# Half of the weight products of a two-layer encoder turned over: activations stationary, 512 weight columns streaming

## The reference: what is computed

```
for i in range(2):
    h = rmsnorm(x, norm_mix_g[i])
    x = x + (even_mixer(h, ...) if i == 0 else diff_attention(h, ...))
    x = x + square(relu(rmsnorm(x, norm_ffn_g[i]) @ w_ff1[i])) @ w_ff2[i]    # 2048 -> 8192 -> 2048
return rmsnorm(x, norm_final_g)
```

## Time and profile before

| what | us |
|---|---|
| median of 3 runs (2211.26 to 2212.45) | 2212.16 |
| the profiled execution's own time | 2212.59 |
| its span in the trace | 2210.8 |
| busy: PE (matmul) / DVE / ACT / POOL | 2182.3 / 1525.7 / 1034.5 / 29.8 |

### The profile page before, as it was taken

One profiled execution on the slowest core, in us unless ns is written; L12 is line 12 of the kernel. 1 busy time (PEld: TensorE's weight loads), 2 busy tenths in 40 slices (PEclk: granted clock), 3 DMA queues, 4 the chain that ended last, 5 costly groups with the idle time before them and its releaser, 6 DMA issues.

```text
span 2210.8 us, 36913 instructions
## 1 busy us (share of the span) xinstructions
PE 2182.3 (99%) x12668; PEld 1909.4 (86%) x12668; DVE 1525.7 (69%) x2296; ACT 1034.5 (47%) x1466; POOL 29.8 (1%) x33
## 2 busy tenths in 40 slices
PE   6999999999999999999999999999999999999998
PEld 5888888888888888888888888888888888888887
DVE  7777767765665675677777777777656656756764
ACT  4444445543443453455545455555434434534553
POOL 3000000000000000000000000000000000000000
PEclk9999999999999999999999999999999999999999
DMA  8444445555555555555544444555555555555552
GB/s 287 171 162 163 170 168 207 197 191 188 190 190 190 189 186 190 182 187 191 185 172 172 163 164 167 173 189 190 190 190 181 192 187 182 189 190 189 190 190 95
DMA packets 64455, 405.65 MB, mean 183 GB/s; under 512 B 6631, under 2 KB 15847, under 8 KB 16396
## 3 DMA queue, kind: packets, MB, share of 16 engines
q1 hardware_dynamic: 61182, 401.06, 50.8%
q10 hardware_dynamic: 2846, 2.82, 0.4%
q0 software_dynamic: 368, 0.99, 0.1%
HBM read 402.70 MB, written 2.14 MB: 183 GB/s over the span
## 4 chain that ended last, share of the span: by engine, by line
issue 78%; PE 20%; DVE 1%; DMA 0%; ACT 0%; POOL 0%; POOLq 0%; SPq 0%; DVEq 0%; ACTq 0%
PE acc L973 12%; PE acc L976 6%; PE ps_scores L1015 0%; DMA x<-xT_dram 0%; PE ps_o L1015 0%; PE ps_aux L1083 0%; PE ps_attn_t L1047 0%; DVE gx L614 0%; ACT gx L341 0%; DVE w_lo L553 0%; PE ps_scores L1070 0%; POOL rstd_col L287 0%; PE ps_v L1036 0%; ACT w_hi L315 0%; POOL bias L212 0%
## 5 line engine op out<-in xcount | busy, mean ns | idle before, releaser
L553 DVE TENSOR_TENSOR w_lo<-raw,w_hi 128x1024 fp32r<-128x1024 f32 x752 | 917.9, 1225 | 321.5 <-ACT w_hi L315 306.9
L973 PE MATMUL acc<-gx,w_hi 128*128 128x512 f32 x3440 | 1088.9, 398 | 10.3 <-DVE gx L614 9.7
L315 ACT ACTIVATE w_hi<-raw 128x1024 fp32r<-128x1024 f32 x752 | 795.7, 1058 | 617.5 <-PE acc L976 613.9
L973 PE MATMUL acc<-mid,w_hi 128*128 128x512 f32 x2544 | 800.1, 396 | 0.3 <-DVE mid L911 0.3
L976 PEld LDWEIGHTS acc<-gx,w_lo 128*128 128x128 f32 x3440 | 648.2, 188 | 153.0
L976 PE MATMUL acc<-gx,w_lo 128*128 128x256 f32 x3440 | 678.1, 279 | 0.0
L976 PEld LDWEIGHTS acc<-mid,w_lo 128*128 128x128 f32 x2544 | 477.9, 188 | 112.9
L973 PEld LDWEIGHTS acc<-gx,w_hi 128*128 128x128 f32 x3440 | 526.4, 189 | 14.3 <-DVE gx L614 8.9
L976 PE MATMUL acc<-mid,w_lo 128*128 128x256 f32 x2544 | 499.8, 278 | 0.0
L973 PEld LDWEIGHTS acc<-mid,w_hi 128*128 128x128 f32 x2544 | 387.6, 189 | 0.8 <-DVE mid L911 0.7
L322 ACT ACTIVATE copied<-acc 128x256 f32<-128x256 f32 x215 | 81.8, 380 | 353.6 <-PE acc L976 349.3
(11 more groups left out here) (123 smaller groups left out, 538.3 us busy)
## 6 DMA issues: line engine op xcount, KB each, us to landing
raw<-weights_dram SPq DMA_DIRECT2D x375, 1024.0 KB, 4.8
x<-xT_dram SPq DMA_DIRECT2D x4, 512.0 KB, 9.2
bias<-bias_line SPq DMA_DIRECT2D x2, 1024.0 KB, 7.2
bias<-bias_line ACTq DMA_DIRECT2D x2, 1024.0 KB, 10.8
out_dram<-bias SPq DMA_DIRECT2D x3, 384.0 KB, 2.9
raw<-weights_dram SPq DMA_DIRECT2D x2, 512.0 KB, 6.2
bias<-bias_line SPq DMA_DIRECT2D x2, 512.0 KB, 6.9
pos_dft<-position_dft_dram POOLq DMA_DIRECT2D x1, 512.0 KB, 8.2
```

Source lines behind the costliest of these rows:

```text
L315: act.activation(w_hi[:, n % RING, :], raw[:, u % RAW_SLOTS, part * HALF:(part + 1) * HALF], ACT.Copy).then_inc(hi_ready, 1)
L553: dve.tensor_tensor(w_lo[:, n % RING, :], raw[:, u % RAW_SLOTS, part * HALF:(part + 1) * HALF], w_hi[:, n % RING, :].bitcast(F32), ALU.sub ...
L973: pe.matmul(acc_of(u)[:], w_hi[:, n % RING, cols], operand[:, kt, :], start=kt == 0, stop=False)
```

## The change

188 of the 376 units are done the other way round: the values of both attentions, both output projections and the down half of both feed-forwards. Such a unit is a quarter of a group of 512 output columns (4 k-tiles x 512 columns, again 1 MB). The activations are stationary, 128 tokens at a time, and the weights stream, 512 columns; each of two banks receives 128 tokens by 512 features:

```
+            def wide_half(n, part, q, operand, banks, o=0, free=(), between=(), done=None, order=range(KT)):
+
+                pe.wait_ge(lo_ready, n + 1 - N0 + 2 * o)
+                for t in range(QT):
...
+                    for i in range(2):
+                        at = 4 * q + 2 * part + i
+                        tile, cols = order[at], slice(i * WIDE, (i + 1) * WIDE)
+                        hi, lo = (operand[:, tile, a * SEQ + t * P:a * SEQ + (t + 1) * P] for a in range(2))
+                        pe.matmul(banks[t], hi, w_hi[:, n % RING, cols], start=at == 0, stop=False)
+                        pe.matmul(banks[t], hi, w_lo[:, n % RING, cols], start=False, stop=False)
+                        ins = pe.matmul(banks[t], lo, w_hi[:, n % RING, cols], start=False, stop=at == KT - 1)
```

The residual x is token-major, `x[P, QT, D]`. A group of 512 columns is added to it from two banks by two DVE instructions, and its squares are summed along the row by ACT. For the three inner norms PE turns the group, and ACT and DVE write gx from the turned tiles:

```
-                    dve.tensor_tensor(x[:, t, :], x[:, t, :], acc_of(u)[:, 0:SEQ], ALU.add).then_inc(acc_half, 1)
-                    dve.wait_ge(acc_half, r + 1 + r_o)
-                    dve.tensor_tensor(x[:, t, :], x[:, t, :], acc_of(u)[:, SEQ:], ALU.add).then_inc(acc_free, 1)
+                        dve.tensor_tensor(x[:, t, columns(g)], x[:, t, columns(g)], banks[g][t], ALU.add
+                                          ).then_inc(x_done, 1)
...
+                act.activation(squares_out, x[:, t, columns(g)], ACT.Square, accum_out=token_parts[:, t, g:g + 1]
...
+            def turn_group(n, group, g):
+                    for j in range(WIDE // P):
+                        cols = slice((WIDE // P * g + j) * P, (WIDE // P * g + j + 1) * P)
+                        for t in range(QT):
+                            ins = pe.transpose(turned_tile(j)[:, t * P:(t + 1) * P], x[:, t, cols], ident[:])
```

The opening is another product: the values of heads 0 to 3, k-tile by k-tile, so that each step needs one tile of x and one 128x512 piece of the weights. Twelve matmuls on ones stand ahead of it. The token-major x is loaded after units 4 and 5, and its squares stand on ACT between the splits of unit 5:

```
+            for c, (lo, hi) in enumerate(CHUNKS):
+                sp.dma_start(raw_open[:, lo:hi, :], opening[:, lo:hi, :]).then_inc(open_landed[c], 16)
+                if c > 1:
+                    sp.dma_start(x_first[:, lo:hi, :], x_fm[:, lo:hi, :]).then_inc(x_landed[c], 16)
+            load(4)
+            load(5)
+            for t in range(QT):
+                sp.dma_start(x[:, t, :], x_tok[:, t, :]).then_inc(tokens_landed[t], 16)
...
+            split_hi(8)
+            split_hi(9)
+            first_squares(0)
+            split_hi(10)
+            first_squares(1)
+            split_hi(11)
...
+            for _ in range(WARM):
+                pe.matmul(ps_aux[:, 0:P], ones[:], ones[:], start=True, stop=True)
+            for kt in range(KT):
+                pe.wait_ge(gx_ready, kt + 1)
+                pe.wait_ge(open_lo, kt + 1)
+                for t in range(QT):
...
+                    pe.matmul(v_banks[0][t], hi, w, start=kt == 0, stop=False)
+                    pe.matmul(v_banks[0][t], hi, w_rest, start=False, stop=False)
+                    ins = pe.matmul(v_banks[0][t], lo, w, start=False, stop=kt == KT - 1)
```

More of the change, by code:

```diff
@@ new lines, in wide_stage @@
+            def wide_stage(u0, g0, n, last=()):
+                for g in range(COL_GROUPS):
+                    for q in range(4):
+                        u = u0 + 4 * g + q
+                        if g == 0:
+                            quarter(u, **last[q])
+                        elif q == 0 and n is not None:
+                            quarter(u, first=[squares(n, g0 + g - 1, g - 1)], second=[turned_hi(n, g - 1)])
+                        else:
+                            quarter(u)
@@ L499, in _, with group @@
-            feed_forward(act, 0, U_FF0, hidden, output, last_output(N_MIX1))
-            unit(U_QKV1)
-            unit(U_QKV1 + 1)
-            def squares(h, oh=0):
-                def step():
-                    act.wait_ge(o_ready, A_HEADS + h + 1 + oh)
-                    act.wait_ge(osq_done, QT * (h + oh))
+                narrow(u, w, o, ow, second=[hi_hidden])
+            def group(u, G, g, m, w, o=0, oG=0, om=0):
+                for q in range(4):
+                    quarter(u + q, o)
@@ new lines, in _ @@
+            end = C_HEADS - 1
+            wide_stage(U_OUT1, G_OUT1, N_FFN1,
+                       (dict(first=[exps(1, A_HEADS + 2 * end + 1, HEADS - 1)]), dict(first=[copy_attn(HEADS - 1)]),
+                        dict(before=[o_squares(end)], first=[hi_att1(end)]), none))
+            norm_end(N_FFN1, G_OUT1 + COL_GROUPS - 1)
+            feed_forward(act, 1, hidden, group)
+            for g in range(COL_GROUPS):
+                for q in range(4):
+                    u = UNITS - KT + 4 * g + q
+                    quarter(u, first=[squares(N_FINAL, G_LAST + g - 1, g - 1)] if g and q == 0 else [], split=u + 2 < UNITS)
@@ L628, in clear_sum, with narrow @@
-            def clear_sum(m=None):
-                if m is not None:
-                    dve.wait_ge(mid_ready, m)
-                dve.memset(sum_sq[:], 0.0).then_inc(sum_steps, 1)
-            def unit(u, evac, o=0, before=(), first=(), then=(), second=(), split=True):
+            def narrow(u, w, evac, o=0, before=(), first=(), second=()):
+                for step in before:
+                    step()
+                split_lo(2 * u + 4, o)
+                for step in first:
+                    step()
+                evac()
+                split_lo(2 * u + 5, o)
+                for step in second:
+                    step()
@@ L635, in unit, with quarter @@
+            def quarter(u, o=0, before=(), first=(), second=(), split=True):
                 for step in before:
@@ new lines, in quarter @@
+            def quarter(u, q, operand, banks, done, o=0, free=(), tiles=None, middle=(), late=(), after=(),
+                        order=range(KT)):
+                for part in range(2):
+                    if tiles is not None:
+                        ready, count = tiles
+                        pe.wait_ge(ready, count + 4 * q + 2 * part + 2)
+                    wide_half(2 * u + part, part, q, operand, banks, o, free if part == q == 0 else (),
+                              late if part else (), done if part == 1 and q == 3 else None, order)
+                    for step in after if part else middle:
+                        step()
```

1518 lines of the change are left out of this document (782 added, 736 removed).

## The result

| what | before | after |
|---|---|---|
| median of 4 runs each, us | 2212.01 (2211.26 to 2212.45) | 2180.60 (2180.37 to 2180.83) |
| ratio, 95% interval | | 0.9858 [0.9841, 0.9875] |
| span of the profiled execution | 2210.8 | 2178.6 |

The changed kernel is 31.4 us faster, 1.4%.

A forecast was written before the change was run, and what follows sets the result against it. PE's matmul stream, with an opening ahead and a tail behind, was taken as the bound. 2212.6 + 3.9 - 12.8 + 2.6 + 2.0 - 2.3 = 2206.0 us, forecast 2206, range 2184 to 2216.

The forecast's parts named there:

- wide products: 188 of 376 units made wide: 24 matmuls of 512 columns at an assumed 0.2331 us each, +3.9 us.
- opening and its waits: Start of the kernel: opening ends at 31 us, then three waits; 11.9 us lost against 24.7, so -12.8.
- small matmuls: On PE: 96 transposes added, 56 turn_v transposes and 16 sum-of-squares matmuls gone, +2.6 us.
- new waits: PE waits on lo_attn in 11 heads, 1 us, and at U_QKV1, 1 us: +2.0 us.
- the end: Last matmul's start to end of span: 10.2 us against 12.5, so -2.3.
- Rival (a): Wide products: a cost per matmul, 512 columns take 0.2290, dropping 1504 matmuls gains 14.5 us, giving 2187.6; chance 0.2.
- the sixteen-row: Row of sixteen 256-column matmuls in succession, 0.119 us each; used for the wide products' lower price, cited for (a).
- (b): Wide products: the 512-column stream from the ring costs 0.236 us, +13.1 us, giving 2219; chance 0.1.
- (c): Opening: clock stays at 1.2 GHz throughout, it ends near 49 us and gains nothing, giving 2219; chance 0.08.
- (d): Wide products: (a)'s mechanism at a quarter of its size, 512 columns take 0.2314 us, giving 2198; chance 0.05.
- The one at U_QKV1: PE waits for the second residual addition before U_QKV1 may start, 1 us.
- The 0.1 in eleven heads: lo_attn, now behind the second split, is 0.1 us late in 11 heads, 1 us in all.

The follow-up runs named there:

- experiment 2: Kernel before, with all eight 512-column w_hi products of a half unit, then its eight 256-column w_lo products, instead of two and two: 2218.04 us (1.0025).
- Experiments 4 and 5: Kernel before, each k-tile pair on mid as three 512-column products, weights streaming (first) or activations streaming (second): 2191.85 and 2191.68 us (both 0.9908).
- Experiment 6: Kernel after, without the twelve warming matmuls on ones ahead of the first product: 2180.74 us (0.9858).
- Experiment 8: Kernel after, channel mixing of heads 9 to 11 moved later and layer 1's first values quarter freed from the second addition to x: 2177.84 us (0.9845).
- experiment 7: Kernel after, with each 512-column product of the wide quarters cut into four of 128 columns: 3157.44 us (1.4274).

## Why the prediction was wrong

The terms, in us, as the prediction had them and as the traces and runs show them:

| term | forecast | measured |
|---|---|---|
| wide products | +3.9 | 4512 x 0.2267 - 1047.8 = -24.9 |
| opening and its waits | -12.8 | 31.07 - 96 x 0.2267 = 9.3 lost, + 0.7 + 1.1 = 11.1 against 24.7: -13.6 |
| small matmuls | +2.6 | 9.50 - 5.47 - 1.46 = +2.6 |
| new waits | +2.0 | 2.0 + 1.0 + 0.6 = 3.6, less 0.8 of this kind before: +2.8 |
| the end | -2.3 | 12.3 - 12.8 = -0.5 |
| sum | -6.6 | -33.6; the spans differ by -32.2 |

**The step that failed** is "I assume that 512 columns keep the price that they have between 512-column neighbours". It is off by 28.8 us, more than the whole error of 25.4. The 0.2331 was measured exactly, but on the first and second product of runs of two, and experiment 2 shows that a run comes to its steady 0.2267 only later: at the sixth product behind eight of 256, at the third behind two. Of the 24.9 us, 1504 products fewer at 13.3 ns are 20.0, and the 3.3 ns that each of the 1504 pairs paid for its changes of width are 5.0. Experiments 4 and 5 show the consequence by itself: 1272 pairs turned into three 512s save 20 us, with either operand streaming.

**Rival (a)** was the right mechanism at less than its size: a fixed cost per matmul, and 1504 fewer of them. It took the cost from a sum of two equations, the sixteen-row and the pair, and the pair is not steady. The sixteen-row alone would have given it: 0.1194 - 0.1067 = 12.7 ns per matmul, so 0.226 for 512 columns and about -28 us. I held against it that "no 512 gap in the pair is that short". That is true and says nothing about a run. Rivals (b), (c) and (d) are refuted: no gap of 0.236 in the long wide stretch (the kernel has some, at starts of runs), the clock high in the opening, and 0.2267 instead of 0.2314. The Trainium skill's 2.5 ns per matmul (TensorE: Matmul & The Clock Gate, "Wait — 56ns, not 53.3ns?") does not agree with this kernel: 13.3 ns here.

**Opening.** The end at 31 us was right to 0.1, partly by luck: the clock was high from the first product (I had put 31 between that case, 29.9, and a late rise, 32.3), and PE starved 0.4 us at the second k-tile and gave 1 us to the product on the bias table at 16.4. Experiment 6 measures the other case, 32.53. The wait for the spread (0.6) did not occur. The wait for v_tok was 0.7 instead of 1.6. The one of 1 us for a load of unit 8 did not occur at a product; a wait of 1.1 for ch_map stood there instead. A load is behind it too: ACT waited 4.0 us for it, until 50.20, and the split, the softmax and the copies of the maps follow in its queue.

**Small matmuls.** The 96 transposes take 9.50 us from start to start, the 56 and the 16 that went took 5.47 and 1.46. Right.

**New waits.** The one at U_QKV1 came as forecast (1.0). The 0.1 in eleven heads did not come, once excepted (0.6). Four of 0.5 that I had not named came: the channel mixing is asked for at the end of the half unit in which its input is evacuated. Experiment 8 takes three of them and 0.65 of the one at U_QKV1 away, and the time falls by 2.8 us, all of it at these places.

**The end.** The prediction's 12.5 for the end before should have been 12.8 (2210.8 - 2197.99). The addition and the square took what I gave them. The power took 1.05 instead of 0.70, the scaling 2.3 instead of 1.7, and the 5.1 us from the end of the scaling were 6.6: before, the stores start while the scaling goes on, now the first is issued 1.1 us before it ends, and 2.1 MB are still to move. This I read from the trace alone; no experiment tests it.

**What stays open.** The sum of the terms is 1.4 us more than the difference of the spans. The table prices every wide product at 0.2267, but 262 of the 4353 gaps between them behind the opening are 0.228 to 0.25, at the starts of runs, and cost 1.5 us more. That is the size of what is missing; the longer gaps behind transposes (0.31 instead of 0.23) are not priced, before or after. Why a run of 512s needs several products to settle, and what the 13.3 ns are, no run here tells. They are not the time of a weight load, which experiment 7 puts at 0.112, far under a 512 product. But every product here has a load of its own, so a cost for each product and one for each load can't be told apart. And the first product of 256 columns behind 512s (113.4) and the first of 128 behind 256s (0.060) carry only about 6.7 ns.

## What to carry to other kernels

Price a stream of instructions from a place where it has run for a while, not from its first members: here a price steady over 358 pairs was off by 3%, since each pair held the same transient. Where PE is the bound and its products are of mixed widths, count matmuls as well as columns, and bring them to the full 512 in long runs, by whichever operand is convenient. And before refining an opening on PE, find the load that the first dependent chain waits for; a faster start is given back there.

## What the runs showed of the hardware

- A product of this kind in a run, each with its own weight load, costs its columns at 2.4 GHz and 13.3 ns, for 256 columns (0.120) as for 512 (0.2267). In a run of 128 columns it costs 0.112, the pace of the loads; the first of such a run, behind products of 256 columns, 0.060.
- Behind eight products of 256 columns the first five of 512 cost 233.3, 235.8, 228.3, 232.5 and 230.8 ns before the gap is 226.7; behind two, only the first two cost more (232 and 231 at 452.13). Alternating one by one, the mean of a 512 and a 256 is 176 instead of 173.
- After the warming matmuls PE idled 1.45 us and was still at 2.4 GHz. Without them the ten gaps until 11.74 are 0.43, the first 0.57: the 1.2 GHz level. The granted clock in the profile's rows reads 1.00 in both cases; only the gaps tell the two levels apart.
- The same power of two columns on POOL took 0.69 to 0.72 us at all five norms before and at the first four after, and 1.05 at the last, where an addition on DVE (L1007) stands beside it. Whether that addition is the cause, no run tests.
